# Hybrid decoder step: pair products of the recurrence in groups of 32 stationary columns

## What is computed

```
def chunk_step(S, xs):                       # per head, chunk by chunk
    qc, kc, vc, gc = xs
    b = cumsum(gc)                           # log decays, summed along tokens
    decay = where(tri, exp(b[t] - b[s]), 0)
    att = einsum('tk,tsk,sk->ts', qc, decay, kc)
    o = att @ vc + (qc * exp(b)) @ S
    S = exp(b_end) * S + (kc * exp(b_end - b)).T @ vc
    return S, o
...
o = o * rsqrt(mean(o**2) + eps) * norm_g * silu(g)
y = o @ w_out
```

## Time and profile before

| | |
|---|---|
| median of 3 runs | 2060.71 us |
| lowest and highest | 2052.65 and 2062.13 us |
| span of the profiled execution | 2054.1 us |
| its own time outside the profiler's span | not listed; taken as the span |
| TensorE busy | 1953.3 us, 95% |
| VectorE busy | 1045.5 us, 51% |
| ScalarE busy | 770.9 us, 38% |
| GpSimd busy | 384.4 us, 19% |
| one head of the recurrence | 39.7 us |

### The profile page before, as it was taken

How to read it: one execution, slowest core, us unless ns; L and a number is a source line. 1 busy time by engine, 2 the same in 40 slices (tenths; PEclk the granted TensorE clock), 3 DMA queues, 4 the chain that set the end, 5 groups by cost and what they waited for, 6 DMA issues and landing times. The chain is left out here.

```text
span 2054.1 us, 46521 instructions
## 1 busy us (share of the span) xinstructions
PE 1953.3 (95%) x19082; PEld 1465.8 (71%) x19082; DVE 1045.5 (51%) x2629; ACT 770.9 (38%) x1683; POOL 384.4 (19%) x424
## 2 busy tenths in 40 slices
PE   7999999989997999997999899899999999999998
PEld 7888888866666778875666344687888778788543
DVE  3111131148874443434766233678777777877332
ACT  0000011158873444433677001355445544544300
POOL 5432333335660000003452100000000000000000
PEclk9999999999998999998999999999999999999999
DMA  6333322444149999997564923599998998998730
GB/s 181 100 124 93 81 66 72 82 94 152 51 161 288 379 380 380 392 371 274 193 241 152 269 67 106 177 282 313 323 312 267 324 302 275 307 313 300 231 133 26
DMA packets 222098, 443.39 MB, mean 216 GB/s; under 512 B 60832, under 2 KB 182193, under 8 KB 205249
## 3 DMA queue, kind: packets, MB, share of 16 engines
q1 hardware_dynamic: 214432, 364.57, 55.4%
q0 software_dynamic: 7456, 75.86, 10.1%
HBM read 413.70 MB, written 165.23 MB: 282 GB/s over the span
## 5 line engine op out<-in xcount | busy, mean ns | idle before, releaser
L2315 PE MATMUL three<-x1T,arena 128*128 128x256 f32 x768 | 204.1, 393 | 0.9 <-DVE rec_qq L2706 0.9
L580 POOL TENSOR_TENSOR late<-late 128x512 f32<-128x512 f32 (+2 forms) x76 | 112.1, 1476 | 220.9 <-PE pab_bZ L368 127.7
L2614 POOL TENSOR_TENSOR rec_v_own<-rec_rows,row_own 64x512 f32<-64x512 f32 x16 | 16.5, 1032 | 717.9 <-PE rec_bX L2429 593.3
L2315 PEld LDWEIGHTS three<-x1T,arena 128*128 128x128 f32 x768 | 135.3, 190 | 15.4 <-DVE rec_qq L2706 1.3
L852 ACT ACTIVATE ap_sc<-ap_sc,ap_nmax 128x256 f32<-128x256 f32 (+1 forms) x192 | 106.3, 557 | 2.4 <-DVE ap_nmax L876 2.3
L1477 DVE COPY sa_kT<-sa_bT 128x512 f32<-128x512 f32 x80 | 55.2, 690 | 94.9 <-PE sa_bT L1333 94.8
L876 DVE CUSTOM_DVE_ANT_0 ap_sc<-ap_bS,ap_bias 128x256 f32<-128x256 f32 (+1 forms) x192 | 86.1, 486 | 12.0 <-DMA ap_bias<-in_bias_p 7.4
L1477 ACT COPY sa_kT<-sa_bT 128x512 f32<-128x512 f32 x80 | 46.9, 586 | 99.0 <-PE sa_bT L1333 98.8
L911 POOL TENSOR_SCALAR ap_sc<-ap_sc,ap_rden,sgl 128x256 f32<-128x256 f32 (+3 forms) x128 | 76.4, 607 | 40.4 <-DVE ap_rden L884 40.2
L1496 DVE COPY sa_xT<-sa_bT 128x512 f32<-128x512 f32 x64 | 43.8, 684 | 66.4 <-PE sa_bT L1398 66.1
L1333 PE MATMUL sa_bT<-ident,arena 64*128 64x64 f32 x1280 | 58.5, 231 | 14.2 <-issue 4.8
(11 more groups left out here) (513 smaller groups left out, 4567.4 us busy)
## 6 DMA issues: line engine op xcount, KB each, us to landing
out<-in_cache_a_k SPq DMA_DIRECT2D x8, 8160.0 KB, 29.6
out<-in_cache_a_v SPq DMA_DIRECT2D x8, 8160.0 KB, 29.4
arena<-in_cache_a_k SPq DMA_DIRECT2D x40, 1024.0 KB, 8.7
arena<-in_cache_a_v SPq DMA_DIRECT2D x40, 1024.0 KB, 9.0
arena<-in_w_in_c SPq DMA_DIRECT2D x64, 512.0 KB, 6.8
late<-in_w_in_ab SPq DMA_DIRECT2D x128, 64.0 KB, 2.4
late<-in_w_in_ab SPq DMA_DIRECT2D x8, 1024.0 KB, 5.4
ap_bias<-in_bias_p SPq DMA_DIRECT2D x16, 512.0 KB, 4.0
```

The lines of the kernel that those rows point to most:

```text
L580: nc.gpsimd.tensor_tensor(to, a, b, op).then_inc(sums, 1)
L2315: last = nc.tensor.matmul(bank[:, 0:SEQ // 2], left[:, k, :], right[:, k, :], start=(first and k == 0), stop=(k == 3), skip_group_check=True)
```

## The change

Near blocks and level 32 stay as they are, in a loop of their own over the tiles. Levels 64 and 128 move behind it, into a loop over pairs of tiles (one even, one odd). Level 128 is cut into two matmuls of 32 keys by 64 queries. For an even tile the blocks go to the same place of `bA` as before. For an odd tile they go to other partitions and columns: level 64 to partitions 32 higher and columns 32 lower, level 128 to partitions 64 higher and columns 64 lower. So four matmuls in a row write to partitions that begin at 0, 32, 64 and 96 in some order. The mask for odd tiles now holds only the four 32x32 blocks of the diagonal, and three more VectorE copies bring the displaced blocks back into `att`, straight from `bA`, after the masked copy has ended.

```diff
-                        for i, width in enumerate(LEVELS):
-                            half = width // 2
-                            for c in range(P // width):
-                                at = m * P + width * c
-                                last = nc.tensor.matmul(bA[width * c:width * c + half, at + half:at + width], far[:, i, at:at + half],
-                                                        far[:, i, at + half:at + width], start=True, stop=True, skip_group_check=True)
+                        for c in range(4):
+                            at = m * P + 32 * c
+                            nc.tensor.matmul(bA[32 * c:32 * c + 16, at + 16:at + 32], far[:, 0, at:at + 16], far[:, 0, at + 16:at + 32],
+                                             start=True, stop=True, skip_group_check=True)
+                    for even in range(0, TILES, 2):
+                        for c in (0, 2):
+                            for m in (even, even + 1):
+                                at = m * P + 32 * c
+                                rows, to = (32 * c, at + 32) if m == even else (32 * c + 32, at)
+                                nc.tensor.matmul(bA[rows:rows + 32, to:to + 32], far[:, 1, at:at + 32], far[:, 1, at + 32:at + 64],
+                                                 start=True, stop=True, skip_group_check=True)
+                        for c in (0, 1):
+                            for m in (even, even + 1):
+                                at, queries = m * P + 32 * c, m * P + 64
+                                rows, to = (32 * c, queries) if m == even else (32 * c + 64, m * P)
+                                last = nc.tensor.matmul(bA[rows:rows + 32, to:to + 64], far[:, 2, at:at + 32], far[:, 2, queries:queries + 64],
+                                                        start=True, stop=True, skip_group_check=True)
...
-                    predicated(0, att[:, :], m_pair[:, :], bA[:, :]).then_inc(att_ready, 1)
+                    line(predicated(0, att[:, :], m_pair[:, :], bA[:, :]))
+                    moved_to, moved_from = (x[:, :].rearrange("p (e odd c) -> p e odd c", e=2, odd=2)[:, :, 1, :] for x in (att, bA))
+                    nc.vector.tensor_copy(moved_to[0:64, :, 64:128], moved_from[64:128, :, 0:64])
+                    for r in (0, 64):
+                        last = nc.vector.tensor_copy(moved_to[r:r + 32, :, r + 32:r + 64], moved_from[r + 32:r + 64, :, r:r + 32])
+                    last.then_inc(att_ready, 1)
...
+    odd = (s <= t) & (s // 32 == t // 32)
+    return {"pair_all": np.tile(np.concatenate([s <= t, odd], axis=1), (1, TILES // 2)).astype(np.int32), ...
```

More of the change, by code:

```diff
@@ L3152, in pair_masks @@
     own = (s // NT == t // NT) & (s <= t)
-    return {"pair_all": np.tile(s <= t, (1, TILES)).astype(np.int32), "pair_own": own.astype(np.int32)}
+    odd = (s <= t) & (s // 32 == t // 32)
+    return {"pair_all": np.tile(np.concatenate([s <= t, odd], axis=1), (1, TILES // 2)).astype(np.int32), "pair_own": own.astype(np.int32)}
 def kernel(**inputs):
```

## The result

The changed kernel takes 2045.66 us in the median of 20 runs (2037.30 to 2057.07), the kernel before 2059.32 us (20 runs, 2052.65 to 2069.28). The ratio is 0.9931, with a 95% interval of 0.9915 to 0.9947: 14 us faster, between 11 and 17.5. The profiled execution spans 2035.4 us instead of 2054.1, 18.7 us less. Forecast were 2040.7 us and a gain of 20 us. Of the 18.7 us, 0.5 lie ahead of the first head's pairs, 17.6 in the 15 stretches between the transposes of one head and the next, and 0.6 behind the last of them. That the runs show less than the profile is the one thing that the prediction had no rival for, and most of the experiments are about it.

The account below looks back on a forecast made before the run. TensorE's order of work was taken to bound each 39.7 us head. Pair products 0.48 + 0.12 + 0.23 + 0.14 = 0.97 us against 2.27; 1.33 us taken, times 15 heads, 20 us: 2060.7 to 2040.7 us, own range 2034 to 2048.

Parts of the forecast that it names:

- What bounds the kernel: In the recurrence, TensorE's order of work sets a head's 39.7 us; what is taken out of it is gained.
- The passages and the overlap: Pair products: passages between four and two column groups cost 0.28 us a tile; level 128 rounds overlap, 0.23 instead of 1.56 us.
- Rival A: Level 128 rounds of 64 columns don't overlap: 0.91 instead of 0.23 us a head, 2051 us in all; chance 0.12.
- rival C: Alternating even and odd tiles at levels 64 and 128 is not overlapped: 4.2 us a head, 2089 us; chance 0.05.
- Rival B: Pair product records cost by number, 25.8 ns each: 96 take 2.48 us a head, 2064 us, no change; chance 0.03.
- the pace and the way out: Pair products: four loads begin in 0.03 us; the passage to product 5 behind them takes 0.14 us a head.
- The line wait: On VectorE before the three copies: costs the masked copy's overlap with its follower, 0.14 us.
- the cover: VectorE's waits around the pairs hide its added work, up to about 2.0 us a head before the reciprocal slips.
- Rival D: VectorE becomes the bound if its added part exceeds about 2.0 us: 2045 us at 2.3 us added; chance 0.04.
- The last head: It gains nothing, as TensorE waits for the output weights, 0.98 growing to about 2.3 us; 15 of 16 heads count.
- DMA's idle time: DMA is at 0.00 between 1901 and 1903 us before a cache copy; a head shorter by 1.33 us fits there.
- rival E: DMA becomes the bound: a backlog of 15 heads before the output weights takes half the gain, 2050 us; chance 0.06.

Follow-up runs that it names:

- wide_last: Kernel before, with the four level 128 matmuls (64 stationary columns) behind all tiles, no displaced blocks; ratio to before 0.9949, head 38.90 us.
- no_copies_back: Changed kernel without the three VectorE copies and the wait before them, displaced blocks left out of `att`; ratio to before 0.9931, head 38.49 us.
- three_copies: Changed kernel with the three VectorE copies made three times over; ratio to before 0.9952, head 38.69 us.
- again: The changed kernel, unaltered, timed and profiled again as control; ratio to before 0.9927, profile span 2050.2 us.
- weights_first: Changed kernel with the last output weights issued before the last cache copies instead of behind them; ratio to before 0.9928, span 2042.5 us.
- rows_later: Changed kernel with each head's cache copies issued once the next pair products are done; median 2042.00 us, ratio to before 0.9928.

## Why the prediction was right, point by point

**What bounds the kernel.** Right. TensorE's order of work sets the length of a head: every microsecond taken out of the pair products came out of the head.

**The passages and the overlap.** Right in mechanism, and the largest term. wide_last isolates the passages: 0.81 us a head. Rival A (rounds of 64 columns don't overlap) and rival C (mixing two tiles stops the overlap) are refuted by the 16 loads of level 128 that stream like the others. Rival B, cost by number, falls with 96 records in 0.85 us. The Trainium skill's rule of about 25 ns from start to start (TensorE: Matmul & The Clock Gate, "Wait — 56ns, not 53.3ns?") would ask 2.4 us (an estimate: 96 x 25 ns); here the trace disagrees.

**Mis-sized: the pace and the way out.** The sum took four loads in 0.03 us from the earlier trace rows for the near blocks and levels 32 and 64, 0.60 us for 80 loads. That pace held for the first 30 loads only, and 78 loads took 0.65 us. The passage to product 5 took 0.20 us instead of 0.14. The rest, level 128, took 0.20 us, about its lower bound of 0.23. Pair products 1.05 us instead of 0.97; the sum's own gain was 1.30, 1.33 was taken, and 1.22 measured. In the kernel before, no more than 20 loads ran without a pause, so its rows could not show this. What sets the slower pace (instructions handed on at that rate once a store of ready ones is used up, or something in the array) was not tried.

**VectorE.** It cost 1.03 us, taken as 0.7 and bounded at 0.86: the bound was wrong. The line wait was 0.14 as worked out, but the copies of 64 elements follow each other after 0.25 us and the first after 0.31, and the little memset ahead of the samples' copy, overlapped before, adds 0.08. The wait in front is 0.82 us where 0.6 was expected, and behind there is none where 0.4 was. The conclusion held, since the cover was named and sized (about 2 us): no_copies_back and three_copies show it from both sides. Rival D falls.

**The last head.** Its own gain was given to the wait for the output weights, 0.98 to 2.35 us in again, as forecast. In the changed kernel's first profile there was no such wait, but 1.7 us went to the half clock shown above. Both vary from run to run, and counting 15 heads of 16 came out about right.

**DMA.** Here the step that failed. It said that a shorter head fits in DMA's idle time and that rival E would show only as a backlog at the end. DMA did not become the bound, but it reached TensorE by a way that the prediction didn't name: TensorE's own instructions come by DMA, and begin some 5 us later beside the cache copies. At the 21 stops TensorE went on 1.2 to 1.6 us after the block had landed. The kernel before shows 0.2 us of such a stop and 0.5 us lost. Four profiles of the changed TensorE program with the cache copies at their old place (changed, again, weights_first, no_copies_back) lost 1.2, 9.3, 8.8 and 13.7 us, 8.3 on average, the half clock behind the longest stops included. 18.3 - 8.3 + 0.5 is 10.5 us, and the runs show 14; four single executions don't give a mean to better than that. The pair without cache copies is 18 us apart.

The forecast was missed by 2045.7 - 2040.7 = 5.0 us. The gain is 13.7 us instead of 20, 6.3 less: 1.7 of it is the pair products' size (15 x 0.11), and the other 4.6 go with the stops, the half clock and the last head. The kernel before came out 1.4 us under the median that the forecast started from, so the time itself is off by only 5.0. That the stops take some 4 us of the gain is the reading that fits the profiles; on the medians alone the difference between 18 and 14 is not clear of the runs' spread. The time still lies in the forecast's own range, 2034 to 2048 us. That the term left out was no larger is luck.

**What stays open.** Why a stop lasts 1.2 to 1.6 us beyond the landing of the block; what a program would do whose blocks end elsewhere, with the same matmuls; what brings the half clock behind the last head in some profiles and not in others; and whether rows_later beats the changed kernel by the 2 to 4 us that were expected of it.

## What to carry to other kernels

Sort small matmuls by how many column groups they use before cutting them: a passage to a wider form and back cost 0.28 us here, more than the matmuls themselves, and moving one loop gave two thirds of the gain. Count instructions as well as columns: where matmuls get shorter and denser, TensorE can run out of loaded instructions under heavy DMA, and a long stop cost clock on top. The sign here was idle time of TensorE that nothing released, with a multiple of 256 instructions from one such stop to the next. And take a second profile before trusting the first; two of the same kernel differed by 15 us here, nearly the whole effect.

## What was not expected of the hardware

- With four column groups in turn, weight loads begin every 7 ns for the first 30, then every 9.7 ns.
- A 16 KB block of instructions takes about 1.1 us to load, and began 6.6 us later in one head when 8 MB copies ran beside it; TensorE then stood still for up to 3.8 us, at the same places of the program in several profiles, and always at the end of a block of 256 instructions.
- With each of the four longest stops (2.62 to 3.77 us) TensorE's granted clock fell to 0.50 for 3.4 us or more: the stop of 3.28 us cost 5.1 us in all.
